# A one-core decoder layer: three query-weight roundings, two inverse roots, the sparse rows and one residual load put at other places in their engines' programs

## The chip, the cores and the metric

The kernel runs on one core of a Trainium2 chip. The metric is the device time of one execution in microseconds (us), the median of several. The core has TensorE (PE in the profile, its weight loads PEld), VectorE (DVE), ScalarE (ACT), GpSimd (POOL) and SyncE (SP), which here only issues DMAs. Each runs its own program in order and waits on semaphores for the others.

## The reference

One layer on 256 tokens of width 2048, float32 throughout. Only the second half matters here:

```python
h = h + concatenate([ret, nsa]) @ w_out[l]
h = h + peer_ffn(rmsnorm(h, norm2_g[l]), peer_wq[l], peer_subkeys[l], peer_u[l], peer_v[l])
return rmsnorm(h, norm_f_g)

def peer_ffn(x, wq, subkeys, u, v):        # x: 256 x 2048
    q = (x @ wq).reshape(n, 8, 2, 128)     # the queries
    s = einsum('nhpd,pkd->nhpk', q, subkeys)
    sv, si = top_k(s, 16)                  # and top 16 of the 16 x 16 sums: 128 experts a token
    hid = gelu(einsum('cd,chkd->chk', x, u[experts]))
    return einsum('chk,chkd->cd', gate * hid, v[experts])
```

u and v hold 16384 rows of 2048 floats each.

## The kernel before

**Weight blocks.** All dense weights arrive as blocks of 1 MB (`raw`, four slots). For an exact product in the fast float format a block is split: ScalarE rounds it into `hi` (`round_static`, `round_lap`; L1072, L1082), VectorE subtracts to get `lo` (`rest_static`, `rest_block`; L1436), and TensorE does three products for each of 16 pieces, 48 matmuls in all (`weights_block`; L585 to L587). `hi` and `lo` have two slots, so the rounding of block m waits until block m - 2 is multiplied (`block_done`). Blocks are numbered through the program: `M_OUT2` (52) begins the second half of the output product, `M_WQ` (60) the 16 blocks of the query weights, `M_PEER` (76) the blocks of u. The text calls the query blocks Q0 to Q15, which are blocks 60 to 75.

**Normalisation.** h is summed up token by token while the output product ends. Its squares are added up and the inverse root is needed in two forms: `rstd`, 128 x 256, made of a TensorE sum over partitions (`spread_sums`, L888, in the middle of Q1), by which VectorE scales each query block's result (`scaled`, L1449) and then h itself (`normalise`, 16 instructions in two groups of 8, L1722); and `rstd_cols`, one column for each half of the tokens, for the 64 sparse tokens. Each takes two activations of ScalarE (`rsqrt`, L1086 and L1088). TensorE may start a query block only when the block two before has been scaled out of its bank (`acc_evacuated`).

**Dense and sparse tokens.** 192 tokens go through all 128 blocks of u and v. For the last 64, GpSimd gathers the chosen rows, and VectorE multiplies them with `xs` (their normalised h) and sums into `acc`; both are filled on partitions 64 to 127 and, from there or by a zero, on 0 to 63. `acc` is set up by a ScalarE copy (L1263) and a VectorE zero (L1731), `xs` by one VectorE instruction (L1733) and a DMA.

**The u blocks of the first half.** 64 blocks of u (`u_block`, L904) are multiplied unsplit. Between blocks 32 and 56 a batch of the gate matrix is built after each (`gate_batch`, L959). After block 60 TensorE opens six banks (L971). ScalarE applies a gelu to each block's result (`hidden_block`, L1273), and after that of block 61 it copies the residual h into the opened banks (L1349, L1351), for which SP has loaded it back from DRAM into `res_back` (L461, L463) where the one-hot tiles of the gate batches stood. Then come 64 blocks of v, split again (`round_split`, L1306; `rest_split`, L1899) and multiplied with the split hidden values `wm` (L1336, L1953, L1954) into all eight banks (`v_block`, L1000 to L1007). The second halves of u and v follow.

**SP's order.** SP asks for the weight blocks in order; the ask for u block r waits until block r - 4 is multiplied. The last lines before the v blocks are:

```python
with sp.Fori(1, HALF // RAW) as lap:
    for s in range(RAW):
        load_after_block(a["u"][RAW * lap + s], RAW * lap + (m_u(0) - RAW + s + 1), s)
sp.wait_ge(gate_rows, BATCHES)
sp.wait_ge(res_stored, 16)
sp.dma_start(res_back[:, 0:1024], res_dram[:, 1024:D]).then_inc(res_loaded, 16)
```

Of the kernel before, what the change touches and what calls it, by code (L numbers as in the profile page):

```python
# [21 lines left out]
ALU = mybir.AluOpType  # L22
ACT = mybir.ActivationFunctionType
AX = mybir.AxisListType

P = 128
T = 256
D = 2048
KT = D // P
# [20 lines left out]
RAW = 4  # L50
# [3 lines left out]
def m_u(half): return M_PEER + 2 * HALF * half  # L54
# [127 lines left out]
def build(nc, a, out):  # L182
    with ExitStack() as ctx:
# [193 lines left out]
        def _(sp):  # L377
# [60 lines left out]
            def load_after_block(src, done, s):  # L438

                sp.wait_ge(block_done, done)  # L440
                sp.dma_start(raw[:, s, :], src).then_inc(raw_loaded[s], 16)
# [6 lines left out]
            for half in range(2):  # L448
                if half:
                    with sp.Fori(0, HALF // RAW) as lap:  # L450
                        for s in range(RAW):
                            load_after_v(a["u"][RAW * lap + (HALF + s)], 2 * RAW * lap + 2 * (HALF - RAW + s + 1), s)
                else:
                    for s in range(RAW):
                        load_after(a["u"][s], M_PEER - RAW + s, s)
                    with sp.Fori(1, HALF // RAW) as lap:
                        for s in range(RAW):
                            load_after_block(a["u"][RAW * lap + s], RAW * lap + (m_u(0) - RAW + s + 1), s)
                    sp.wait_ge(gate_rows, BATCHES)
                    sp.wait_ge(res_stored, 16)  # L460
                    sp.dma_start(res_back[:, 0:1024], res_dram[:, 1024:D]).then_inc(res_loaded, 16)  # L461
                    for x in range(2):
                        sp.dma_start(res_back[TS * x:TS * (x + 1), 1024:3072], res_dram[0:TS, D:2 * D]).then_inc(res_loaded, 16)  # L463

                def load_v(mv, s):
                    if half == 0 and mv < RAW:
                        load_after_block(a["v"][:, mv, :], m_v(0) - RAW + mv + 1, s)
                    else:
                        load_after_v(a["v"][:, mv + HALF * half, :], 2 * (mv + 2 * HALF * half - RAW + 1), s)

                def load_gates(q, g):
                    sp.dma_start(gs[:, g, 0:TD * GROUP_J], gate_dram[q].rearrange("i t j -> i (t j)")).then_inc(gate_loaded[g], 16)

                early = GATED_EARLY // GROUP_J if half == 0 else 0
                first = 0 if half == 0 else HALF // GROUP_J - GATED_EARLY // GROUP_J
                for q in range(early):
                    for r in range(GROUP_J):
                        load_v(GROUP_J * q + r, r % RAW)
                    if q == 1:
                        for s in range(2):  # L480
                            sp.wait_ge(gate_stored[s], 16 * (TD // 32))
                        for g in range(2):
                            load_gates(g, g)
                for q in range(early, HALF // GROUP_J):
                    if half and q == 3:
                        sp.wait_ge(block_done, m_v(1) + 8)
                        sp.dma_start(h_first, res_dram[:, 0:1024]).then_inc(gf_loaded, 16)
                    x = first + q - early
                    if x >= 2:
                        sp.wait_ge(gated, GROUP_J * (x - 1))  # L490
                        load_gates(x, x % 2)
                    for r in range(GROUP_J):
                        load_v(GROUP_J * q + r, r % RAW)
# [17 lines left out]
        def _(pool):  # L511
# [19 lines left out]
            pool.wait_ge(acc_evacuated, M_WQ)  # L531
            pool.dma_start(g2_row[TS:P, :], a["norm2_row"]).then_inc(sparse_loaded, 16)
            pool.dma_start(res_dram, res).then_inc(res_stored, 16)
            pool.wait_ge(xs_ready, 1)
            pool.dma_start(xs[0:TS, :], xs[TS:P, :]).then_inc(sparse_loaded, 16)

            pool.wait_ge(picked_ready, 1)
# [526 lines left out]
        def _(ac):  # L1064
# [9 lines left out]
            def round_static(m):  # L1074
                n = raw_at(m)
                round_block(m, m, n % RAW, n // RAW + 1)
# [7 lines left out]
            def rsqrt(src, dst, width, logged, ready, count, rows=P):  # L1084

                do(dst, src, ACT.Ln, bias=eps[0:rows, :], scale=1.0 / width).then_inc(logged, 1)  # L1086
                ac.wait_ge(logged, count)
                do(dst, dst, ACT.Exp, scale=-0.5).then_inc(ready, 1)  # L1088
# [146 lines left out]
            def square_h(c):  # L1235

                ac.wait_ge(acc_evacuated, M_OUT2 + 2 * c + 2)
                for tt in range(2):
                    at = (2 * c + tt) * 512
                    do(qT[:, at:at + 512], res[:, tt * D + c * 512:tt * D + (c + 1) * 512], ACT.Square,  # L1240
                       accum_out=ss_parts[:, 4 * tt + c:4 * tt + c + 1]).then_inc(sq_ready, 1)
# [13 lines left out]
            for x in range(2):  # L1255
                copy_h(3, x)
                round_h(3, x).then_inc(act_hi_ready, 1)
            square_h(3)
            ac.wait_ge(sq_summed, 2)
            rsqrt(ss_cols, rstd_cols, D, log_ready, rstd_ready, 2)  # L1260
            ac.wait_ge(ss_ready, 2)
            rsqrt(bank[7][:, 0:T], rstd[:, :], D, log_ready, rstd_ready, 3)
            do(acc[TS:P, :], h_sparse, ACT.Copy).then_inc(acc_begun, 1)  # L1263
            for s in range(2, RAW):
                round_static(M_WQ + s)
            with ac.Fori(1, KT // RAW) as lap:
                for s in range(RAW):
                    round_lap(RAW * lap + (M_WQ + s), lap, s, (M_WQ + 8) // RAW + 1)

            def hidden_block(r):  # L1270

# [18 lines left out]
                do(sc[:, 1 - x // 4, 4 * (x % 4):4 * (x % 4) + 4, :].rearrange("p g k -> p (g k)"),  # L1290
                   bank[2 + x % 6][:, :], ACT.Copy).then_inc(q_copied, 1)
            ac.wait_ge(res_stored, 16)
            ac.wait_ge(xs_ready, 1)
            hidden_block(0)

            def round_split(n):
# [134 lines left out]
        def _(dv):  # L1431
# [292 lines left out]
            for s in range(2, RAW):  # L1724
                rest_static(M_WQ + s)
                if s == 2:
                    dv.wait_ge(rstd_ready, 3)
                    scaled(M_WQ, 0, qT[:, 0:T])
                scaled(M_WQ + s - 1, s - 1, qT[:, (s - 1) * T:s * T])
                normalise((0, 8)[s - 2], (8, KT)[s - 2])  # L1730
            vec.memset(acc[0:TS, :], 0.0).then_inc(acc_begun, 1)  # L1731
            dv.wait_ge(sparse_loaded, 16)
            vec.scalar_tensor_tensor(out=xs[TS:P, :], in0=h_sparse, scalar=rstd_cols[TS:P, 1:2], in1=g2_row[TS:P, :],  # L1733
                                     op0=ALU.mult, op1=ALU.mult).then_inc(xs_ready, 1)
            with dv.Fori(1, KT // RAW) as lap:
                for s in range(RAW):
                    rest_block(RAW * lap + (M_WQ + s), s, s)
                    scaled(RAW * lap + (M_WQ + s - 1), s - 1, qT[:, bass.ds(RAW * T * lap + (s - 1) * T, T)])
            scaled(M_PEER - 1, 1, qT[:, (KT - 1) * T:KT * T])

            done = {"route": 0, "items": 0}
# [301 lines left out]
```

## Time and profile before

| | |
|---|---|
| median of 3 runs | 1823.74 us (1823.47 to 1824.27) |
| the profiled execution | 1824.49 us, of which the span of its instructions is 1822.7 us |
| TensorE matmul, weight load | 1787.2 us (98%), 1615.2 us (89%) |
| VectorE, ScalarE, GpSimd | 76%, 42%, 9% of the span |
| mean granted TensorE clock | 0.994 |
| DMA | 531 MB, mean 291 GB/s |

A span is the time from the first to the last instruction. Matmuls overlap: each one's row lasts longer than the distance to the next, so TensorE's rate is read from how many start in a stretch. "Idle before" and the arrow name the instruction or DMA that ended a wait.

### The profile page before, as it was taken

What the parts mean: (1) busy time and instruction counts of PE and PEld (TensorE: products, weight loads), DVE (VectorE), ACT (ScalarE), POOL (GpSimd) and SP (SyncE); (2) the same over time, 40 slices, a digit from 0 to 9 for tenths busy, and PEclk for the clock granted to TensorE, in tenths of its full rate; (3) what the DMA queues carried; (4) which work ended last, traced back from release to release, by engine and by line L of the source; (5) the groups of instructions that cost most, each with busy time, mean ns of one, the idle gap of its engine ahead of it and who ended that gap; (6) DMA issues with size and microseconds to landing.
All of it is one profiled execution on the core that took longest, in us unless ns stands there. A gap on an engine that the chain in (4) does not pass through costs nothing.

```text
span 1822.7 us, 28601 instructions
## 1 busy us (share of the span) xinstructions
PE 1787.2 (98%) x10988; PEld 1615.2 (89%) x10988; DVE 1389.8 (76%) x2156; ACT 770.0 (42%) x1060; POOL 172.2 (9%) x157
## 2 busy tenths in 40 slices
PE   8999999998999999999999999999999999999997
PEld 8999999788899999999977777789999998777775
DVE  6546667565539896887458888989999998998996
ACT  5234445655221101111145555555555555554555
POOL 0000000000000112222210001011111111010110
PEclk9999999999999999999999999999999999999999
DMA  9674443555444898889899999999999999999984
GB/s 350 234 280 160 163 139 116 208 185 201 168 156 167 309 337 317 314 330 341 333 343 368 323 319 329 351 339 368 380 369 376 374 366 346 351 365 361 362 305 151
DMA packets 77136, 531.07 MB, mean 291 GB/s; under 512 B 8796, under 2 KB 9196, under 8 KB 15997
## 3 DMA queue, kind: packets, MB, share of 16 engines
q1 hardware_dynamic: 54080, 377.44, 55.9%
q0 software_dynamic: 22352, 151.59, 22.8%
q8 instruction: 48, 0.79, 0.2%
q10 hardware_dynamic: 620, 0.96, 0.2%
q14 instruction: 36, 0.29, 0.0%
HBM read 512.60 MB, written 15.20 MB: 290 GB/s over the span
## 4 chain that ended last, share of the span: by engine, by line
PE 94%; DVE 2%; DMA 1%; issue 1%; ACT 1%; SPq 0%; ACTq 0%; DVEq 0%
PE bank L904 17%; PE bank L920 11%; PE bank L585 8%; PE bank L586 7%; PE bank L587 7%; PE bank L1001 6%; PE bank L1000 6%; PE bank L1005 6%; PE bank L1006 6%; PE bank L1007 6%; PE bank L921 5%; PE bank L959 2%; DMA raw<-in_v 1%; DVE lo L1436 0%; PE bank L712 0%
## 5 line engine op out<-in xcount | busy, mean ns | idle before, releaser
L1899 DVE TENSOR_TENSOR lo<-raw,hi 128x1024 fp32r<-128x1024 f32 x384 | 463.8, 1222 | 113.4 <-ACT hi L1306 112.9
L1306 ACT ACTIVATE hi<-raw 128x1024 fp32r<-128x1024 f32 x384 | 404.8, 1059 | 325.8 <-PE bank L1007 241.4
L904 PE MATMUL bank<-hT,raw 128*128 128x192 f32 x2048 | 337.5, 326 | 0.0
L904 PEld LDWEIGHTS bank<-hT,raw 128*128 128x128 f32 x2048 | 332.3, 190 | 0.1
L920 PE MATMUL bank<-xr,hi 128*128 128x384 f32 x1024 | 291.3, 359 | 0.0
L1436 DVE TENSOR_TENSOR lo<-raw,hi 128x2048 fp32r<-128x2048 f32 x75 | 171.8, 2291 | 111.2 <-ACT hi L1072 78.9
L921 PE MATMUL bank<-xr,lo 128*128 128x192 f32 x1024 | 256.4, 250 | 0.0
L1000 PE MATMUL bank<-hi,wm 128*128 128x512 f32 x512 | 200.9, 392 | 6.2 <-DVE wm L1954 5.7
L1001 PE MATMUL bank<-lo,wm 128*64 128x512 f32 x512 | 203.6, 398 | 0.0
L1005 PE MATMUL bank<-lo,wm 128*128 128x512 f32 x512 | 201.0, 393 | 0.0
L1006 PE MATMUL bank<-hi,wm 128*128 128x512 f32 x512 | 199.9, 390 | 0.0
L1007 PE MATMUL bank<-hi,wm 128*128 128x512 f32 x512 | 199.9, 390 | 0.0
L585 PE MATMUL bank<-act,hi 128*128 128x256 f32 x672 | 195.4, 291 | 2.1 <-DVE lo L1436 1.9
L921 PEld LDWEIGHTS bank<-xr,lo 128*128 128x128 f32 x1024 | 196.0, 191 | 0.0
L920 PEld LDWEIGHTS bank<-xr,hi 128*128 128x128 f32 x1024 | 192.4, 188 | 0.0
L586 PE MATMUL bank<-act,hi 128*128 128x256 f32 x672 | 191.1, 284 | 0.0
L587 PE MATMUL bank<-act,lo 128*128 128x256 f32 x672 | 191.1, 284 | 0.0
L1771 DVE SCALAR_TENSOR_TENSOR rows_sb<-rows_sb,xs 128x2048 f32<-128x2048 f32 x64 | 146.3, 2286 | 20.0 <-DMA rows_sb<-in_u_rows,pairs 19.8
L1774 DVE SCALAR_TENSOR_TENSOR acc<-rows_sb,wcol,acc 128x2048 f32<-128x2048 f32 x64 | 150.2, 2347 | 9.8 <-DMA rows_sb<-in_v,pairs 9.2
L1273 ACT ACTIVATE arena<-bank 128x192 f32<-128x192 f32 x64 | 21.1, 329 | 285.2 <-PE bank L904 285.2
L585 PEld LDWEIGHTS bank<-act,hi 128*128 128x128 f32 x672 | 129.8, 193 | 6.7 <-issue 6.0
L1000 PEld LDWEIGHTS bank<-hi,wm 128*128 128x128 f32 x512 | 96.7, 189 | 43.8 <-issue 10.0
(296 smaller groups left out, 2629.3 us busy)
## 6 DMA issues: line engine op xcount, KB each, us to landing
raw<-in_u SPq DMA_DIRECT2D x128, 1024.0 KB
raw<-in_v SPq DMA_DIRECT2D x128, 1024.0 KB
raw<-in_w_in SPq DMA_DIRECT2D x44, 1024.0 KB
raw<-in_w_out SPq DMA_DIRECT2D x16, 1024.0 KB
raw<-in_wq SPq DMA_DIRECT2D x16, 1024.0 KB
gate_matrix<-gs POOLq DMA_DIRECT2D x12, 768.0 KB, 12.2
gs<-gate_matrix SPq DMA_DIRECT2D x12, 768.0 KB
raw<-in_cmp_w SPq DMA_DIRECT2D x8, 1024.0 KB
```

The lines of the kernel that those rows point to most:

```text
L585: mm(dst, wh, mh, start=first, stop=False)
L586: mm(dst, wh, ml, start=False, stop=False)
L587: return mm(dst, wl, mh, start=False, stop=last)
L904: last = mm(bank[s % 2][:, 0:TD], raw[:, s, k * P:(k + 1) * P], xn[:, k, 0:TD], start=(k == 0), stop=(k == KT - 1))
L920: mm(acc_bank[:, 0:2 * TD], hi[:, s % 2, w], xr[:, k, :], start=(k == 0), stop=False, skip_group_check=True)
L921: last = mm(acc_bank[:, 0:REST_COLS], lo[:, s % 2, w], xr[:, k, 0:REST_COLS], start=False, stop=(k == KT - 1), skip_group_check=True)
L1000: mm(bank[4 + dc][:, :], packed, vh[:, cols], start=False, stop=False, skip_group_check=True)
L1001: return mm(bank[4 + dc][0:TS, :], packed[:, 0:TS], vl[:, cols], start=False, stop=closing, skip_group_check=True)
L1005: mm(bank[dc][:, :], whole, vl[:, cols], start=opening and dc < 2, stop=False, skip_group_check=True)
L1006: mm(bank[dc][:, :], whole, vh[:, cols], start=False, stop=False, skip_group_check=True)
L1306: do(hi[:, s % 2, cols], raw[:, s, cols], ACT.Copy).then_inc(v_hi_ready, 1)
L1899: vec.tensor_tensor(lo[:, n % 2, cols], raw[:, n % RAW, cols], hi[:, n % 2, cols].bitcast(F32), ALU.subtract).then_inc(v_lo_ready, 1)
```

## The change

ScalarE, between the output product and the query blocks: the rounding of Q2 is put ahead of `rstd`'s root, the rounding of Q3 ahead of `rstd_cols`'s root (which was first), and the copy into `acc` behind all query blocks. VectorE: the zero of `acc` is gone, and `xs` is made in four parts of 512 columns, one behind each of the last four query blocks' roundings and scalings (those four are taken out of the loop). GpSimd writes the zeros. SP asks for the residual after the ask for u block 60 and before those for 61, 62 and 63.

```diff
@@ block.sync
-                    with sp.Fori(1, HALF // RAW) as lap:
+                    with sp.Fori(1, HALF // RAW - 1) as lap:
                         for s in range(RAW):
                             load_after_block(a["u"][RAW * lap + s], RAW * lap + (m_u(0) - RAW + s + 1), s)
+                    load_after_block(a["u"][HALF - RAW], m_u(0) + HALF - 2 * RAW + 1, 0)
                     sp.wait_ge(gate_rows, BATCHES)
                     sp.wait_ge(res_stored, 16)
                     sp.dma_start(res_back[:, 0:1024], res_dram[:, 1024:D]).then_inc(res_loaded, 16)
                     for x in range(2):
                         sp.dma_start(res_back[TS * x:TS * (x + 1), 1024:3072], res_dram[0:TS, D:2 * D]).then_inc(res_loaded, 16)
+                    for s in range(1, RAW):
+                        load_after_block(a["u"][HALF - RAW + s], m_u(0) + HALF - 2 * RAW + s + 1, s)
@@ block.gpsimd
             pool.dma_start(res_dram, res).then_inc(res_stored, 16)
-            pool.wait_ge(xs_ready, 1)
+            nc.gpsimd.memset(acc[0:TS, :], 0.0).then_inc(acc_begun, 1)
+            pool.wait_ge(xs_ready, 4)
             pool.dma_start(xs[0:TS, :], xs[TS:P, :]).then_inc(sparse_loaded, 16)
@@ block.scalar
             square_h(3)
+            round_static(M_WQ + 2)
+            ac.wait_ge(ss_ready, 2)
+            rsqrt(bank[7][:, 0:T], rstd[:, :], D, log_ready, rstd_ready, 2)
+            round_static(M_WQ + 3)
             ac.wait_ge(sq_summed, 2)
-            rsqrt(ss_cols, rstd_cols, D, log_ready, rstd_ready, 2)
-            ac.wait_ge(ss_ready, 2)
-            rsqrt(bank[7][:, 0:T], rstd[:, :], D, log_ready, rstd_ready, 3)
-            do(acc[TS:P, :], h_sparse, ACT.Copy).then_inc(acc_begun, 1)
-            for s in range(2, RAW):
-                round_static(M_WQ + s)
+            rsqrt(ss_cols, rstd_cols, D, log_ready, rstd_ready, 3)
             with ac.Fori(1, KT // RAW) as lap:
                 for s in range(RAW):
                     round_lap(RAW * lap + (M_WQ + s), lap, s, (M_WQ + 8) // RAW + 1)
+            do(acc[TS:P, :], h_sparse, ACT.Copy).then_inc(acc_begun, 1)
@@ block.vector
                 if s == 2:
-                    dv.wait_ge(rstd_ready, 3)
+                    dv.wait_ge(rstd_ready, 2)
                     scaled(M_WQ, 0, qT[:, 0:T])
                 scaled(M_WQ + s - 1, s - 1, qT[:, (s - 1) * T:s * T])
                 normalise((0, 8)[s - 2], (8, KT)[s - 2])
-            vec.memset(acc[0:TS, :], 0.0).then_inc(acc_begun, 1)
-            dv.wait_ge(sparse_loaded, 16)
-            vec.scalar_tensor_tensor(out=xs[TS:P, :], in0=h_sparse, scalar=rstd_cols[TS:P, 1:2], in1=g2_row[TS:P, :],
-                                     op0=ALU.mult, op1=ALU.mult).then_inc(xs_ready, 1)
-            with dv.Fori(1, KT // RAW) as lap:
+            with dv.Fori(1, KT // RAW - 1) as lap:
                 for s in range(RAW):
                     rest_block(RAW * lap + (M_WQ + s), s, s)
                     scaled(RAW * lap + (M_WQ + s - 1), s - 1, qT[:, bass.ds(RAW * T * lap + (s - 1) * T, T)])
+            dv.wait_ge(sparse_loaded, 16)
+            dv.wait_ge(rstd_ready, 3)
+            for s in range(RAW):
+                r = KT - RAW + s
+                rest_block(M_WQ + r, s, s)
+                scaled(M_WQ + r - 1, s - 1, qT[:, (r - 1) * T:r * T])
+                cols = slice(s * 512, (s + 1) * 512)
+                vec.scalar_tensor_tensor(out=xs[TS:P, cols], in0=h_sparse[:, cols], scalar=rstd_cols[TS:P, 1:2], in1=g2_row[TS:P, cols],
+                                         op0=ALU.mult, op1=ALU.mult).then_inc(xs_ready, 1)
```

ScalarE's later wait for `xs_ready` goes from 1 to 4. TensorE's program is the same.

ScalarE, where the output product ends and the query blocks begin, before the change. L1240 squares the last part of h, the pairs L1086 and L1088 are the two roots, L1263 is the copy into `acc`, L1072 the roundings of Q2 and Q3:

```order
L1240 ACTIVATE arena,small<-arena 128x512
L1086 ACTIVATE small<-small 128x2 [waits sq_summed]
L1088 ACTIVATE small<-small 128x2 [waits log_ready]
L1086 ACTIVATE rstd<-bank,small 128x256 [waits ss_ready]
L1088 ACTIVATE rstd<-rstd 128x256 [waits log_ready]
L1263 ACTIVATE acc<-arena 64x2048
L1072 ACTIVATE hi<-raw 128x2048 [waits block_done,raw_loaded2]
L1072 ACTIVATE hi<-raw 128x2048 [waits block_done,raw_loaded3]
```

The same place in the changed kernel, where its lines have other numbers (L1076 rounds, L1090 and L1092 are a root):

```order
L1244 ACTIVATE arena,small<-arena 128x512
L1076 ACTIVATE hi<-raw 128x2048 [waits block_done,raw_loaded2]
L1090 ACTIVATE rstd<-bank,small 128x256 [waits ss_ready]
L1092 ACTIVATE rstd<-rstd 128x256 [waits log_ready]
L1076 ACTIVATE hi<-raw 128x2048 [waits block_done,raw_loaded3]
L1090 ACTIVATE small<-small 128x2 [waits sq_summed]
L1092 ACTIVATE small<-small 128x2 [waits log_ready]
L1269 UNCONDITIONAL_BRANCH
```

Q2's rounding now stands ahead of the wait for `ss_ready`, Q3's between the roots, and no copy follows.

VectorE, from the second group of 8 normalising instructions (L1722) to the first block of the loop (Q4), before:

```order
L1449 TENSOR_TENSOR arena<-bank,rstd 128x256 [waits block_done]
L1722 TENSOR_TENSOR hT<-hT,rstd 128x256 x8
L1731 MEMSET acc 64x2048
L1733 SCALAR_TENSOR_TENSOR xs<-arena,small,g_row 64x2048 [waits sparse_loaded]
L1735 UNCONDITIONAL_BRANCH
L1735 ISA
L1436 TENSOR_TENSOR lo<-raw,hi 128x2048 [waits hi_ready]
```

And changed:

```order
L1453 TENSOR_TENSOR arena<-bank,rstd 128x256 [waits block_done]
L1726 TENSOR_TENSOR hT<-hT,rstd 128x256 x8
L1735 UNCONDITIONAL_BRANCH
L1735 ISA
L1440 TENSOR_TENSOR lo<-raw,hi 128x2048 [waits hi_ready]
```

The zero and the `xs` instruction are gone from between Q3 and Q4; the latter is now four instructions of 64x512 behind Q12 to Q15.

SP, at the end of the first u blocks, before:

```order
L441 DMA raw<-in_u 128x2048
L456 REGISTER_ALU
L456 COMPARE_AND_BRANCH
L461 DMA res_back<-residual 128x1024 [waits res_stored,gate_rows]
L463 DMA res_back<-residual 64x2048 x2
L441 DMA raw<-in_v 128x2048 [waits block_done] x4
```

And changed:

```order
L456 COMPARE_AND_BRANCH
L441 DMA raw<-in_u 128x2048 [waits block_done]
L462 DMA res_back<-residual 128x1024 [waits res_stored,gate_rows]
L464 DMA res_back<-residual 64x2048 x2
L441 DMA raw<-in_u 128x2048 [waits block_done] x3
L441 DMA raw<-in_v 128x2048 [waits block_done] x4
```

The three residual DMAs stand ahead of three asks for u blocks, each of which waits for one more block.

## Rows read from the trace of the kernel before

**Rows 1.** The page, part 4: the chain that ended last, by engine

```profile
PE 94%; DVE 2%; DMA 1%; issue 1%; ACT 1%; SPq 0%; ACTq 0%; DVEq 0%
```

**Rows 2.** TensorE's waits, whole span: us in total, times, longest us

```profile
PE bank L585 <- DVE lo L1436: 6.8, 3, 4.5
PE bank L1000 <- DVE wm L1954: 5.7, 3, 4.5
PE bank L585 <- DVE arena L1449: 4.8, 1, 4.8
```

**Rows 3.** Timeline of TensorE: start us, us, instruction, [idle before]

```profile
448.33 0.55 PE L585 MATMUL bank<-h_parts,hi 128*128 128x256 f32 x1 [4.76 <-DVE arena L1449]
465.90 0.58 PE L585 MATMUL bank<-h_parts,hi 128*128 128x256 f32 x1 [4.47 <-DVE lo L1436]
```

**Rows 4.** Stretches: PE, PEld, DVE, ACT, POOL busy (instructions), clock, DMA, GB/s

```profile
448.40:451.20 2.80, 2.80 (x13) 2.80 (x14) 2.80 (x10) 0.00 (x0) 0.00 (x0) 0.50 0.69 234
466.00:471.80 5.80, 5.80 (x27) 5.80 (x28) 2.19 (x1) 0.00 (x0) 0.00 (x0) 0.50 0.97 345
480.00:528.00 48.00, 48.00 (x402) 48.00 (x401) 22.16 (x17) 16.90 (x9) 0.00 (x0) 1.00 0.54 187
927.40:932.60 5.20, 5.20 (x12) 3.76 (x13) 2.70 (x4) 2.04 (x4) 0.00 (x0) 0.50 1.01 421
1000.00:1030.00 30.00, 30.00 (x133) 23.27 (x132) 23.77 (x35) 15.66 (x21) 1.87 (x2) 1.00 0.91 326
```

**Rows 5.** Timeline of ScalarE around the end of Q1

```profile
440.74 0.47 ACT L1086 ACTIVATE rstd<-bank,small 128x256 f32<-128x256 f32 x1 [3.20 <-PE bank L888]
441.68 1.91 ACT L1263 ACTIVATE acc<-arena 64x2048 f32<-64x2048 f32 x1
443.62 3.71 ACT L1072 ACTIVATE hi<-raw 128x2048 fp32r<-128x2048 f32 x2
```

**Rows 6.** Timeline of VectorE, Q2 to Q4

```profile
445.56 2.29 DVE L1436 TENSOR_TENSOR lo<-raw,hi 128x2048 fp32r<-128x2048 f32 x1 [8.07 <-ACT hi L1072]
...
455.72 0.42 DVE L1449 TENSOR_TENSOR arena<-bank,rstd 128x256 f32<-128x256 f32 x1 [2.32 <-PE bank L587]
456.06 2.77 DVE L1722 TENSOR_TENSOR hT<-hT,rstd 128x256 f32<-128x256 f32 x8
459.18 1.76 DVE L1731 MEMSET acc<- 64x2048 f32 x1 [0.36 <-issue]
460.98 2.35 DVE L1733 SCALAR_TENSOR_TENSOR xs<-arena,small,g_row 64x2048 f32<-64x2048 f32 x1
```

**Rows 7.** Timeline of GpSimd, its last issue before the changed place

```profile
431.85 0.58 POOL L533 DMA_DIRECT2D residual<-arena  x1
```

**Rows 8.** Timeline of TensorE, last u blocks and first v block

```profile
884.88 20.97 PE L904 MATMUL bank<-hT,raw 128*128 128x192 f32 x128
...
927.37 0.77 PE L1000 MATMUL bank<-hi,wm 128*128 128x512 f32 x1 [4.54 <-DVE wm L1954]
```

**Rows 9.** Timeline of ScalarE there

```profile
912.47 0.33 ACT L1273 ACTIVATE arena<-bank 128x192 f32<-128x192 f32 x1 [6.26 <-PE bank L904]
919.51 1.12 ACT L1349 ACTIVATE bank<-res_back 128x512 f32<-128x512 f32 x2 [6.70 <-DMA res_back<-residual]
920.56 2.14 ACT L1351 ACTIVATE bank<-res_back 128x512 f32<-128x512 f32 x4
...
923.23 2.00 ACT L1306 ACTIVATE hi<-raw 128x1024 fp32r<-128x1024 f32 x2 [0.28 <-DMA raw<-in_v]
```

**Rows 10.** SP's issues there

```profile
901.41 0.33 SPq L461 DMA_DIRECT2D res_back<-residual  x1
...
905.88 0.34 SPq L441 DMA_DIRECT2D raw<-in_v  x1
```

**Rows 11.** Two stretches there; columns as in rows 4

```profile
889.00:894.00 5.00, 5.00 (x33) 5.00 (x32) 1.22 (x1) 1.09 (x3) 4.08 (x3) 1.00 0.54 172
901.00:923.00 22.00, 21.84 (x132) 21.28 (x131) 4.69 (x5) 4.12 (x10) 4.91 (x3) 1.00 1.02 390
```

More of the change, by code:

```diff
@@ L1292, in _ @@
             ac.wait_ge(res_stored, 16)
-            ac.wait_ge(xs_ready, 1)
+            ac.wait_ge(xs_ready, 4)
             hidden_block(0)
```

## The prediction

> **What bounds the kernel now.** I read the chain that ended last first: 94% of it is TensorE [rows 1], so only what shortens TensorE's own time or its waits can count. Second, TensorE's waits over the whole span [rows 2]: three kinds, 17.3 us in all, and each kind's longest is nearly all of it: 4.5, 4.5 and 4.8 us. Third, where these three lie [rows 3, 8]: 4.76 us before 448.33 (the start of Q2), 4.47 us before 465.90 (the start of Q4), 4.54 us before 927.37 (the start of the first v block). Sum 13.77 us. Fourth, TensorE's pace behind each [rows 4]. After the first, 13 matmuls start in 2.80 us; after the second, 27 in 5.80; in an undisturbed stretch 402 in 48.00, or 0.119 us each. After the third it is 12 in 5.20 us against 133 in 30.00, or 0.226 each. The granted clock column says why: 0.50 in the three stretches, the lower of the two levels (1.2 against 2.4 GHz), and 1.00 in the others; ahead of each TensorE had stood idle for over 4 us. So every idle stretch has a second price: 2.80 - 13 x 0.119 = 1.25, 5.80 - 27 x 0.119 = 2.59, and 5.20 - 12 x 0.226 = 2.49 us. Sum 6.3 us.
>
> **The start of Q2.** Who is late? VectorE scales Q0 and Q1 out of their banks only behind Q2's `lo` (2.29 us at 445.56), which waits for ScalarE's rounding at 443.62, and that stands behind the root for `rstd` (440.74) and the copy into `acc` (441.68, 1.91 us) [rows 5, 6]. Yet ScalarE sat idle for 3.20 us before 440.74, from 437.54, and Q0, which the rounding waits for, was multiplied by about then: TensorE ended Q1 at 448.33 - 4.76 = 443.57, and a block is 48 x 0.119 = 5.7 us, with four small sums besides. Changed, the rounding (half of 3.71, so 1.9 us) fills that idle time: 437.5 to 439.4. `lo` follows until 441.7, VectorE having been idle since 445.56 - 8.07 = 437.49. `rstd` comes when it did, at 441.68, so Q0 is scaled by 442.2, and TensorE wants to start Q2 at 443.57. The wait of 4.76 us is gone, with its slow stretch.
>
> **The start of Q3 and Q4.** What is late next is VectorE's chain behind each scaling. The rows give it as it was for Q4: scaling from 455.72, eight normalising instructions until 456.06 + 2.77 = 458.83, then a pause of 0.36, the zero (1.76) and `xs` (2.35), and Q4's `lo` after 463.33 [rows 6]. TensorE started 0.28 us after that `lo` ended. Without the zero and `xs` the `lo` goes from 458.83 to 461.12, and TensorE could start at 461.40; it had run out of work at 465.90 - 4.47 = 461.43 [rows 3]. So the second wait closes almost exactly. The same chain now decides Q3 too (ScalarE rounds Q3 from 443.6 to 445.5, VectorE scales, scales Q1 at about 443.8, and 461.12 - 455.72 = 5.4 us on, at 449.2, `lo` is there, just when TensorE is through with Q2). I charge 0.2 us for each of the two. Bounds: nothing, and 0.2 + 0.36 each if the pause before the zero comes with the loop's branch. From Q5 on no normalising is left and VectorE has slack.
>
> **Where the moved work goes.** ScalarE's `rstd_cols` root, two activations on 2 columns, now behind Q3's rounding, is under 1 us before an idle stretch. The copy into `acc` (1.91 us) falls behind Q15's rounding, where ScalarE has nothing to do until TensorE has multiplied Q15 and the first u block. The four parts of `xs` (each about 2.35 / 4 = 0.6 us) follow VectorE's 2.29 + 0.42 in a block of 5.7 us: over 2 us to spare. They cost the path nothing; without that cover 2.4 us. GpSimd now waits for the fourth part before its `xs` DMA, and behind this wait stand the gathers, which need the routing of all 64 tokens, tens of us later. Its zero starts behind the issue at 431.85 [rows 7], with no other work on that engine. No GpSimd arithmetic is in this trace; nearest is VectorE's 1.76 us for the same tile, and I take its effect as zero (see the rivals).
>
> The Trainium skill (SBUF — State Buffer, Who interferes with whom) says that VectorE and GpSimd share a port pair as an exclusive lock: a GpSimd instruction that only writes does not stop a VectorE one with two SBUF inputs, but can hold up `tensor_scalar` in its two-port mode until it is over. No run here shows it. By the first half the sum stands; by the second only the two `tensor_scalar` that prepare the sum for `rstd` could be late, which is the last rival below.
>
> **The first v block.** ScalarE, after the gelu of u block 61 (912.47), waited 6.70 us for the residual, until 919.51, and copied it for 3.2 us, so the gelu of block 62 and the first rounding of v came at 922.6 and 923.23 [rows 9]; from that rounding to TensorE's start it is 927.37 - 923.23 = 4.14 us. TensorE was free at 927.37 - 4.54 = 922.83 [rows 8]. The residual was asked for at 901.41, the first v block at 905.88 and used 17.35 us later [rows 10]. From 901 to 923 the DMA engines are full, at 390 GB/s [rows 11], so these two waited behind other transfers. Changed, SP issues the residual when the last gate batch is done. This is where the run of four u blocks starts, 884.88, each 20.97 / 4 = 5.24 us: at some 885.1, or 16.3 us sooner. Part of its 1.57 MB falls into a stretch where the engines are half idle (889 to 894: 0.54, 172 GB/s).
>
> Is it in time? ScalarE wants it at 912.8; it has 27 us where it took up to 18. Then the copies end at 916.1, block 62's gelu follows its end (922.83 - 5.24 = 917.6) at 917.9, the rounding of v starts at 918.2 and TensorE could start at 922.4, before 922.83, if v has landed by 918.2. Its queue carries u60, residual, u61, u62, u63 and v0, 6.8 MB from 885.1; if gathers and gate stores took half of 390 GB/s all the time it would land at 920; at the full rate it would land some 5 us after its ask, at 911. I take in between, about 915: the gathers do not run all the time. So the third wait of 4.54 us and its slow stretch go. The second v block is then next: its rounding waits for the end of u63 and one gelu, and 3.8 us of splitting stand against 20 x 0.226 = 4.5 us of the first v block; I charge 0.1 us.
>
> **The sum.** 13.77 + 6.33 = 20.1 us off, 0.5 us on. Idle is counted from a matmul's modelled end, about 0.16 us after its successor could have started (0.28 against 0.12), three times, which gives 0.4 back. Net 20.0. The profiled execution took 1824.49 us, 0.75 above the median of the runs, and the waits are the program's, so I take them off the median: 1823.74 - 20.0 = 1803.7 us. TensorE has only 1.2 us of other waits behind 927 [rows 2], so nothing there swallows it.
>
> **Rivals.**
> - The first v block still lands late. For: 17.35 us from ask to use before. Against: the residual no longer stands ahead of it. At the bound of 920 TensorE starts at 924.1, 1.3 us idle, and if the clock falls all the same 2.5 more: 1807.5. Chance 0.13.
> - The chain through Q3 and Q4 is longer than its rows (loop branch, wake-ups), and the clock falls once or twice: some 1 us idle and 2.6 us slow, each: 1807 to 1811. For: the margin is 0.03 us. Against: the 0.36 us ahead of the zero is the only pause inside the chain. Chance 0.10.
> - Given back: the v stage is bound by DMA (share 0.91 from 1000 to 1030 [rows 4]), and starting earlier only waits later: 1823.7. Against: TensorE does not wait there, and a transfer is asked for by blocks done. Chance 0.02.
> - Slower: the zero on GpSimd holds VectorE's preparation of the `rstd` sum. It starts at 432.4; VectorE was done with the preparation at 437.49, TensorE's sum comes at about 440, and `rstd` has 1.5 us more, so it costs nothing up to some 8.6 us and from there us for us. It ends on the slower side only beyond 8.6 + 20, about 29 us, 16 times VectorE's 1.76. At 33 us, say, it would be 1803.7 + 24.4 = 1828.1. Chance 0.02.
>
> A residual queued ahead of u61 could also stall TensorE, but 3.7 MB at half of 390 GB/s is 19 us from 885.1, and u61 is wanted at about 907.
>
> **The numbers.** The forecast holds with 0.73, between 1802 and 1805.5. With the first two rivals the range is 1801.5 to 1811, which leaves out well under 2 in 10. A change of 0.2%, 3.6 us, is what this measurement can tell from none. Faster by more: forecast and first two rivals, 0.96; within: 0.02; slower: 0.02.
>
> **What would show it.** In the changed profile TensorE should have no wait over 1 us between 430 and 930, the granted clock 1.00 in all stretches from there to the end, Q2 start near 443.5, the first u block some 13.6 us sooner than before, ScalarE's copies of the residual start right behind block 61's gelu, and VectorE's `lo` of Q4 directly behind the eight normalising instructions. I am wrong if a wait of some us reappears at Q3, Q4 or the first or second v block, or if a low clock shows without a wait before it.

## The result and the profile after

The changed kernel takes 1803.72 us (median of 4 runs, 1802.99 to 1805.51) against 1824.01 us (4 runs, 1823.47 to 1824.36) on the same chip: ratio 0.989, interval 0.9873 to 0.9908, 20.3 us less. The profiled execution took 1804.10 us, its span is 1802.3 us, its mean granted clock 0.998.

TensorE's waits over the whole span, as in [rows 2] (us in total, times, longest):

```profile
PE bank L675 <- DMA arena<-in_window_tables: 7.1, 1, 7.1
PE bank L589 <- DVE arena L1453: 2.0, 1, 2.0
PE bank L1004 <- DVE wm L1963: 1.2, 2, 0.6
...
PE bank L589 <- DVE lo L1440: 0.4, 1, 0.4
```

The three waits of 4.5 to 4.8 us are gone. The first line is a wait at the start, which stood at 6.7 before; the second is one of 1.9 to 2.0 us at 66 us, which was among the 6.8 of [rows 2] and was left alone.

ScalarE at the end of Q1, as in [rows 5] (start, duration, instruction, idle before):

```profile
437.64 1.92 ACT L1076 ACTIVATE hi<-raw 128x2048 fp32r<-128x2048 f32 x1 [0.69 <-PE bank L591]
440.90 0.47 ACT L1090 ACTIVATE rstd<-bank,small 128x256 f32<-128x256 f32 x1 [1.35 <-PE bank L892]
441.41 0.42 ACT L1092 ACTIVATE rstd<-rstd 128x256 f32<-128x256 f32 x1
443.83 1.92 ACT L1076 ACTIVATE hi<-raw 128x2048 fp32r<-128x2048 f32 x1 [2.01 <-PE bank L591]
```

Q2's rounding fills the idle time ahead of the root. The root starts at 440.90 where it was 440.74, but so does all around it in this execution (VectorE's row at 430.36 now stands at 430.52), so the root is not held up. VectorE there, as in [rows 6]:

```profile
439.58 2.29 DVE L1440 TENSOR_TENSOR lo<-raw,hi 128x2048 fp32r<-128x2048 f32 x1 [1.92 <-ACT hi L1076]
441.86 0.42 DVE L1453 TENSOR_TENSOR arena<-bank,rstd 128x256 f32<-128x256 f32 x1
443.77 0.42 DVE L1453 TENSOR_TENSOR arena<-bank,rstd 128x256 f32<-128x256 f32 x1 [1.49 <-PE bank L591]
444.11 2.77 DVE L1726 TENSOR_TENSOR hT<-hT,rstd 128x256 f32<-128x256 f32 x8
446.79 2.29 DVE L1440 TENSOR_TENSOR lo<-raw,hi 128x2048 fp32r<-128x2048 f32 x1
449.53 0.42 DVE L1453 TENSOR_TENSOR arena<-bank,rstd 128x256 f32<-128x256 f32 x1 [0.45 <-PE bank L591]
449.87 2.77 DVE L1726 TENSOR_TENSOR hT<-hT,rstd 128x256 f32<-128x256 f32 x8
452.55 2.29 DVE L1440 TENSOR_TENSOR lo<-raw,hi 128x2048 fp32r<-128x2048 f32 x1
```

`lo` follows the eight normalising instructions at once. From scaling to the end of `lo` the chain is 449.08 - 443.77 = 5.31 us, against the predicted 5.4; the 0.36 us pause ahead of the zero did not come with the loop's branch.

The second place: SP's issues, as in [rows 10], then ScalarE, as in [rows 9], and TensorE, as in [rows 8]:

```profile
869.80 0.34 SPq L441 DMA_DIRECT2D raw<-in_u  x1
871.58 0.33 SPq L462 DMA_DIRECT2D res_back<-residual  x1
...
876.78 10.73 SPq L441 DMA_DIRECT2D raw<-in_u  x3
892.38 17.30 SPq L441 DMA_DIRECT2D raw<-in_v  x4
```

```profile
898.96 0.33 ACT L1277 ACTIVATE arena<-bank 128x192 f32<-128x192 f32 x1 [6.24 <-PE bank L908]
899.19 1.11 ACT L1353 ACTIVATE bank<-res_back 128x512 f32<-128x512 f32 x2
900.23 2.15 ACT L1355 ACTIVATE bank<-res_back 128x512 f32<-128x512 f32 x4
904.16 0.33 ACT L1277 ACTIVATE arena<-bank 128x192 f32<-128x192 f32 x1 [1.79 <-PE bank L908]
904.39 1.99 ACT L1310 ACTIVATE hi<-raw 128x1024 fp32r<-128x1024 f32 x2
```

```profile
893.73 15.60 PE L908 MATMUL bank<-hT,raw 128*128 128x192 f32 x95
909.47 0.47 PE L1004 MATMUL bank<-hi,wm 128*128 128x512 f32 x1
```

The residual copies stand right behind block 61's gelu, and the first v matmul has no listed wait. But VectorE is not as it was; the rows that its items of the sparse tokens wait for come later:

```profile
889.23 2.35 DVE L1783 SCALAR_TENSOR_TENSOR acc<-rows_sb,wcol,acc 128x2048 f32<-128x2048 f32 x1 [12.50 <-DMA rows_sb<-in_v,pairs]
899.94 2.29 DVE L1780 SCALAR_TENSOR_TENSOR rows_sb<-rows_sb,xs 128x2048 f32<-128x2048 f32 x1 [8.36 <-DMA rows_sb<-in_u_rows,pairs]
...
904.19 2.29 DVE L1780 SCALAR_TENSOR_TENSOR rows_sb<-rows_sb,xs 128x2048 f32<-128x2048 f32 x1 [1.95 <-DMA rows_sb<-in_u_rows,pairs]
...
906.41 2.36 DVE L1908 TENSOR_TENSOR lo<-raw,hi 128x1024 fp32r<-128x1024 f32 x2
...
908.89 0.22 DVE L1963 TENSOR_TENSOR wm<-arena,wm 128x64 fp32r<-128x64 f32 x1
```

Before, the same three items began at 898.74, 907.98 and 912.48, the last of them with block 61's gelu (912.47 in [rows 9]); now the last begins 5.2 us behind that gelu (898.96), and the first `lo` of v waits for VectorE itself. `wm` ends at 909.11, and the first v matmul starts 0.36 us behind it. That is the distance in the runs in which TensorE waits for it (927.01 to 927.37 before), so there is no slack left here, though no wait is listed: waits are counted from modelled ends, and the last u matmul's is 909.33. Where `wm` is ready sooner (the changed kernel measured again, below), the first v matmul starts 0.29 us ahead of that end and not 0.14 us behind it. By this comparison, an estimate, some 0.4 us are lost here.

### The profile page after: what moved, and what is told of

Same layout as the page of the kernel before. It is cut to its first block, busy times and chain, and to the rows that moved or that the text cites. A ratio compares the mean times of both kernels' runs of the same rounds, so it can differ in the third digit from the quotient of the medians.

```text
span 1802.3 us, 28580 instructions
## 1 busy us (share of the span) xinstructions
PE 1780.0 (99%) x10988; PEld 1608.9 (89%) x10988; DVE 1389.0 (77%) x2158; ACT 770.1 (43%) x1060; POOL 174.1 (10%) x158
## 4 chain that ended last, share of the span: by engine, by line
PE 96%; DVE 2%; issue 1%; ACT 1%; DMA 0%; SPq 0%; ACTq 0%; DVEq 0%
PE bank L908 18%; PE bank L924 11%; PE bank L589 8%; PE bank L590 7%; PE bank L591 7%; PE bank L1005 6%; PE bank L1004 6%; PE bank L1009 6%; PE bank L1010 6%; PE bank L1011 6%; PE bank L925 5%; PE bank L963 2%; PE bank L716 0%; PE bank L942 0%; PE bank L769 0%
## 5 line engine op out<-in xcount | busy, mean ns | idle before, releaser
L1076 ACT ACTIVATE hi<-raw 128x2048 fp32r<-128x2048 f32 x55 | 105.0, 1909 | 66.7 <-PE bank L591 57.5
```

## The experiments

The kernel before took 1824.5 us (9 runs) on the chip of the first four, 1825.74 (9) on that of the next four, and 1823.97 (7) on that of the last three.

**The query part alone.** The changed kernel with SP's order as before:

```diff
-                    with sp.Fori(1, HALF // RAW - 1) as lap:
+                    with sp.Fori(1, HALF // RAW) as lap:
...
-                    for s in range(1, RAW):
-                        load_after_block(a["u"][HALF - RAW + s], ...)
```

> The changed kernel with the residual asked for as before, behind the last u block; only ScalarE's, VectorE's and GpSimd's edits stand. My theory (three independent waits, two of them at the start of Q2 and Q4): both query waits and their slow-clock stretches are gone, 4.76 + 4.47 + 1.25 + 2.59 + 0.3 less 0.4, so 13.0 us under before, 1811.0 us; the wait of 4.5 us before the first v block and its slow stretch stay. Rival (given back: work saved early is lost again at the crowded DMA queue before the v stage): less than 10 us, with a v wait grown beyond 5 us. Second rival (the gathers, not the residual, hold the first v block up): same time as my theory, but VectorE's last gathered item before the v blocks comes where it did relative to the u blocks.

1809.5 us (5 runs, 1809.11 to 1811.51), ratio 0.9921 (0.9908 to 0.9935): 15.0 us less. TensorE's waits behind `wm`:

```profile
PE bank L1001 <- DVE wm L1960: 5.7, 3, 4.6
```

The query waits are gone and that of the first v block stands. It came out 1.5 us faster than expected. Around the wait, in the profiled execution (1809.36 us), the low clock shows in 913.9 to 917.3, 3.4 us, all of it with TensorE at work. In the kernel before it lasted 6.8 us (925.9 to 932.7), but TensorE started only at 927.37, so 5.3 us of it counted. Stretches, columns as in [rows 4]:

```profile
913.50:917.50 4.00, 4.00 (x12) 2.96 (x11) 2.70 (x4) 1.44 (x4) 0.00 (x0) 0.57 1.00 418
917.50:921.00 3.50, 3.50 (x17) 2.70 (x16) 1.48 (x2) 2.15 (x3) 0.00 (x0) 1.00 1.04 433
```

Half of 5.3 less 3.4 us is an estimated 0.9 us of the gap. Another 0.4 us are the query terms of 1.25 and 2.59, which were too small (see the slow stretches below). The five times fall into 1809.1 to 1809.5 and 1811.3 to 1811.5. Whether the length of the low clock makes these two groups is not shown: only one of the five was profiled.

**The residual part alone.** The kernel before with the new order of SP's issues and nothing else.

> The kernel before with only the residual's ask moved ahead of u blocks 61 to 63. My theory: the v wait of 4.54 us and the slow stretch of 2.49 go, 0.1 comes, so 6.9 us under before, 1817.0 us; both query waits stay, with the clock at 0.50 behind each. Rival (the two parts help each other): the sum of this run's and the query part's gain is off the 20.3 us of both by over 1.5 us. In the profile I look for the gathers: with the residual in the queue earlier, VectorE's last two gathered items should come about 5 us later against the u blocks than before, as in the changed kernel, and the first v block's lo behind them within 0.3 us of TensorE's need.

1817.89 us (5 runs, 1817.05 to 1818.07), 0.9962 (0.9948 to 0.9976): 6.6 us less. With the 15.0 above that is 21.6; the whole change gave 20.3 and, measured again, 21.35. The parts add up as far as these runs can tell: each interval above is some 5 us wide. Both query waits stand in its profile, 4.5 and 4.8 us at the longest. VectorE ahead of the first v block:

```profile
902.55 2.35 DVE L1777 SCALAR_TENSOR_TENSOR acc<-rows_sb,wcol,acc 128x2048 f32<-128x2048 f32 x1 [12.66 <-DMA rows_sb<-in_v,pairs]
913.31 2.29 DVE L1774 SCALAR_TENSOR_TENSOR rows_sb<-rows_sb,xs 128x2048 f32<-128x2048 f32 x1 [8.41 <-DMA rows_sb<-in_u_rows,pairs]
...
917.32 2.29 DVE L1774 SCALAR_TENSOR_TENSOR rows_sb<-rows_sb,xs 128x2048 f32<-128x2048 f32 x1 [1.71 <-DMA rows_sb<-in_u_rows,pairs]
```

Block 61's gelu is at 912.13 here, so the last item begins 5.2 us behind it, as in the changed kernel; with the query part alone it began 0.1 us behind (898.36 against 898.25). The earlier residual is what makes the gathered rows late.

**ScalarE's order alone.** The kernel before with the new order of roundings and roots; the zero and `xs` stay on VectorE between Q3 and Q4.

```diff
+            round_static(M_WQ + 2)
             ac.wait_ge(ss_ready, 2)
-            for s in range(2, RAW):
-                round_static(M_WQ + s)
+            rsqrt(bank[7][:, 0:T], rstd[:, :], D, log_ready, rstd_ready, 2)
+            round_static(M_WQ + 3)
```

> The kernel before with only ScalarE's order changed (roundings of Q2 and Q3 first, copy into acc last); VectorE still zeroes acc and makes xs in one piece between Q3 and Q4. My theory: the wait before Q2 (4.9 with the modelled end) and its slow stretch (1.25) go; the one before Q4 stays at 4.5 to 4.7 us, since 0.36 + 1.76 + 2.35 = 4.47 us of VectorE work stand before Q4's lo, with 2.6 us of slow clock: 6.2 us under before, 1817.6 us. Rival (the two query waits are one lateness handed on, so that curing the first cures part of the second): 9 to 13 us under before.

1817.0 us (4 runs, 1816.51 to 1818.55), 0.9961 (0.9945 to 0.9976). Q2's wait alone is gone; that of the first v block is 3.9 us here instead of 4.5. Q4's stays, and VectorE shows what holds it:

```profile
452.44 1.76 DVE L1731 MEMSET acc<- 64x2048 f32 x1 [0.37 <-issue]
454.24 2.35 DVE L1734 SCALAR_TENSOR_TENSOR xs<-arena,small,g_row 64x2048 f32<-64x2048 f32 x1
456.62 2.29 DVE L1436 TENSOR_TENSOR lo<-raw,hi 128x2048 fp32r<-128x2048 f32 x1
```

**The zero back on VectorE.** The changed kernel with the zero where it stood.

```diff
-            nc.gpsimd.memset(acc[0:TS, :], 0.0).then_inc(acc_begun, 1)
...
+            vec.memset(acc[0:TS, :], 0.0).then_inc(acc_begun, 1)
             with dv.Fori(1, KT // RAW - 1) as lap:
```

> The changed kernel with the zero of acc back on VectorE between Q3 and Q4 instead of on GpSimd. My theory of the margin (Q4's lo has under 0.3 us to spare): TensorE waits 1.76 + 0.36 = 2.1 us more before Q4. If the clock stays at its upper level through a wait of 2.1 us the time is 1803.7 + 2.1 = 1805.8 us; if it falls as it did behind the waits of over 4 us, 2.6 more: 1808.4 us. Rival (VectorE has slack there): 1803.7 us, no wait.

1807.34 us (4 runs, 1806.75 to 1808.18), 0.9906 (0.9891 to 0.9922), so 3.6 us over the changed kernel (3.1 if each is taken against the kernel before on its own chip). Of that 1.9 us is the wait it brings back ahead of Q4 (TensorE's timeline), behind which the clock stayed high (second stretch). The rest need not be the zero's: the profiled execution, the fastest of the four, had its low clock at 67.3 to 70.7 (first stretch), behind the old wait at 66 us, where neither the kernel before nor the changed one showed any.

```profile
458.19 0.38 PE L588 MATMUL bank<-h_parts,hi 128*128 128x256 f32 x1 [1.91 <-DVE lo L1439]
```

```profile
67.40:70.60 3.20, 3.20 (x17) 3.20 (x17) 0.80 (x1) 0.00 (x0) 0.00 (x0) 0.50 1.02 383
458.40:461.40 3.00, 3.00 (x26) 3.00 (x26) 2.15 (x1) 0.00 (x0) 0.00 (x0) 1.00 0.78 227
```

**The changed kernel again.**

> The changed kernel itself once more, beside the variants of this call and to see how its own runs scatter (1802.99 to 1805.51 us so far). If the scatter is the clock's (a low stretch that follows a wait of 2 us near 66 us in some executions and not in others), single runs lie at about 1803.5 or 1.5 to 2 us above, and the profile shows a stretch at 0.50 only where the run is above. If it is the first v block's, which had 0.2 us to spare, slower runs have a wait there.

1804.39 us (4 runs, 1803.49 to 1804.98), 0.9885 (0.987 to 0.99). The profiled execution (1804.38 us) shows neither cause named above: the clock is 1.00 behind the wait at 66 us, and the first v matmul (909.72) is 0.56 us behind `wm`, so not held by it. What spreads the runs over 1.5 us stays open.

```profile
908.94 0.22 DVE L1963 TENSOR_TENSOR wm<-arena,wm 128x64 fp32r<-128x64 f32 x1
909.72 0.53 PE L1004 MATMUL bank<-hi,wm 128*128 128x512 f32 x1
```

**The zero eight times.** GpSimd writes the zeros eight times, each after the last.

```diff
+            for x in range(7):
+                nc.gpsimd.memset(acc[0:TS, :], 0.0).then_inc(osq_ready, 1)
+                pool.wait_ge(osq_ready, x + 2)
             nc.gpsimd.memset(acc[0:TS, :], 0.0).then_inc(acc_begun, 1)
```

> The changed kernel with GpSimd writing the zeros eight times over, one after the other (8 x 1.83 us, from 432.6 to about 447.5), so that they lie beside VectorE's two small instructions on one SBUF input (437.2), the scaling and the normalising. My theory: VectorE's instructions keep their lengths and the time is 1803.7 us. Rival (the shared port pair as an exclusive lock, as in the Trainium skill's page SBUF — State Buffer, Who interferes with whom): the two tensor_scalar each wait for up to one zero, 1.8 us, the sum for rstd comes up to 2.4 us later than at 440.9, and TensorE waits up to 1 us before Q2: 1804 to 1806 us.

1803.38 us (4 runs, 1803.02 to 1804.34), 0.9881 (0.9865 to 0.9896): no cost. Its GpSimd, and VectorE in 432 to 446 by groups (line, operation, count, busy us, mean ns, idle before):

```profile
432.49 13.04 POOL L538 MEMSET acc<- 64x2048 f32 x7
445.58 1.80 POOL L540 MEMSET acc<- 64x2048 f32 x1
```

```profile
L1443 DVE TENSOR_TENSOR lo<-raw,hi 128x2048 fp32r<-128x2048 f32 x2 | 4.6, 2293 | 1.5 <-ACT hi L1079 1.5
L1729 DVE TENSOR_TENSOR hT<-hT,rstd 128x256 f32<-128x256 f32 x6 | 2.1, 418 | 0.0
L1724 DVE TENSOR_SCALAR wmt<-base,small 128x128 f32<-128x128 f32 x2 | 1.1, 994 | 0.0
```

The instructions with two inputs in SBUF take what they took alone (2293 and 418 ns; 2293 and 420 in the changed kernel). The two `tensor_scalar` that prepare the `rstd` sum take 994 ns on average against 285 and end at 438.2 us, just when the third of the eight zeros, begun at 436.24, is over. This is what the Trainium skill (SBUF — State Buffer, Who interferes with whom) says of both kinds; the trace agrees. In the changed kernel the one zero ran from 432.60 to 434.43 and these two started at 437.18, so there they did not meet. The hold costs nothing: VectorE then waits for ScalarE until 439.47 in any case, and the root for `rstd` starts at 440.79, no later than without the seven extra zeros (440.90).

**The residual one block later.** Asked for behind the ask for u block 61 in place of 60.

```diff
-                    load_after_block(a["u"][HALF - RAW], ...)
+                    for s in range(2):
+                        load_after_block(a["u"][HALF - RAW + s], ...)
```

> The changed kernel with the residual asked for one weight block later (behind the ask for u block 61, so two blocks sooner than before instead of three). My theory: it is wanted behind block 61's gelu, some 22 us after this ask, and takes 10 to 17: no new wait, 1803.7 us; the gathered rows that come in while it is loaded move too, so VectorE's last two items before the v blocks shift by up to 5 us against those of the changed kernel. Rival (each block counts: the queue is full, and the first v block lands later by what the residual is later): TensorE waits 1 to 3 us before the first v block, 1805 to 1808 us.

1809.58 us (5 runs, 1805.95 to 1809.91), 0.991 (0.9896 to 0.9923). The expectation was wrong; the rival named in it (each block counts) fits the profiled execution and its wait of 1.2 us. In that execution (1805.95 us) the residual is in time, but the v block that is queued behind it is not:

```profile
907.31 2.00 ACT L1311 ACTIVATE hi<-raw 128x1024 fp32r<-128x1024 f32 x2 [1.89 <-DMA raw<-in_v]
```

```profile
911.46 0.46 PE L1005 MATMUL bank<-hi,wm 128*128 128x512 f32 x1 [1.21 <-DVE wm L1964]
```

It is rounded 7.4 us behind block 61's gelu (899.89), against 5.4 in the changed kernel. VectorE's last item still begins 4.6 us behind that gelu (904.49). Three runs took a further 3.7 us; none of them was profiled, so why stays open.

**The row items one block later.** The 24 items of this stage are spread over one more weight block (`HALF - 3` for `HALF - 4`, line 88).

> The changed kernel with the pace of the gathers in u blocks 32 to 60 stretched by one block, so that the last gathered item before the v blocks is asked for one block (5.2 us) later. In the changed kernel's profile VectorE did that item until 906.5 us and the first v block's lo behind it until 908.8, with TensorE's need at 909.3. My theory: this item, and no longer the residual or the first v block's landing, is what comes last there, so TensorE now waits 3 to 6 us before the first v block, with a low clock behind it of 1.5 to 2.6 us: 1808 to 1812 us. Rival (there is slack; VectorE's wait for the item is filled otherwise): 1803.7 us.

1808.98 us (4 runs, 1807.7 to 1810.29), 0.9913 (0.9898 to 0.9928). The size is as expected, the mechanism is not: TensorE waits 0.9 us for the first v block and 2.8 us for a weight block of u, and the clock stays at 1.00 behind both. Its waits, then the place:

```profile
PE bank L908 <- DMA raw<-in_u: 2.8, 1, 2.8
```

```profile
896.33 8.88 PE L908 MATMUL bank<-hT,raw 128*128 128x192 f32 x53 [2.77 <-DMA raw<-in_u]
```

VectorE's last item begins at 905.40, only 1.2 us later than in the changed kernel, and the first `lo` of v waits for ScalarE's rounding, which waits for the landing. So here the weight loads come last, not the item. The mean share of the DMA engines does not foretell it: in 865 to 875 it is 0.98 where the changed kernel has 0.73, but it is 0.98 in the next experiment too, which has no wait for a u block.

**The row items two blocks sooner.** `HALF - 6`.

> The changed kernel, with the 24 row items of its second stage spread over weight blocks that end two blocks sooner, so that VectorE's last items before the first v block fall sooner. If VectorE's last item is what now comes last ahead of the first v block (it ended at 906.41 us, and TensorE could first go on at 909.3 us), then this has no wait to take away but gives the place slack: 1803.5 us, scatter no larger than in the changed kernel, the item ends by about 901 us, and the first v block starts at block 61's end. If it is the transfers as a whole that are just in time there (the 16 DMA engines read 1.00 to 1.02 from 875 us on), asking for rows sooner pushes back the u blocks instead: a wait for a u weight block appears, 1 to 3 us, and the time is 1805 to 1808 us.

1803.91 us (4 runs, 1803.24 to 1805.77), 0.9889 (0.9873 to 0.9906): no change. VectorE's last item is done at 893.74, and then it idles until v has been rounded, which now waits for the landing:

```profile
907.19 2.00 ACT L1310 ACTIVATE hi<-raw 128x1024 fp32r<-128x1024 f32 x2 [1.66 <-DMA raw<-in_v]
```

TensorE waits 1.0 us. Of the first theory the item and the time came true, but not the start without a wait; the wait for a u block of the second did not come. With the items out of the way the landing of v ends last. It comes at 907.2, where in the changed kernel v was there by 904.4 (0.8 us of the difference stand ahead of the last u blocks already). So rows asked for sooner seem to push back a load, as the second theory has it, but v's and not one of u. The profiled execution, the slowest of the four, again had a low clock at 67.1 to 70.5.

**Four additions moved to GpSimd.** The changed kernel with half of the eight additions that VectorE makes at 59.77 us given to GpSimd, which is idle before and makes them as soon as their inputs are there, at 41.79 us.

```diff
-                    for kind in range(2):
+                    for kind in range(1):
...
+            for g in range(GROUPS):
+                pool.wait_ge(acc_evacuated, VC + g + 1)
+                for lh in range(2):
+                    nc.gpsimd.tensor_tensor(blk[:, 1, ...], rows_of[...], pe_cols[...], ALU.add)
```

> The changed kernel, with four of the eight additions that VectorE makes at 59.77 us (3.95 us for the eight) made by GpSimd. In every profile so far TensorE waits 1.9 us at about 66 us for the low part of the weight block that VectorE makes behind them. If these additions are the cause, half of them gone brings that low part 1.97 us sooner and the wait goes: 1801.8 us (1801.2 to 1802.5). If the weight block is held by something else (ScalarE's high part at 64.33 us, or the transfer), the time stays at 1803.7 us and the wait is there with another releaser. If GpSimd slows VectorE, which works beside it there, the low parts between 60 and 70 us read longer than 2.29 us each and less is gained.

1801.9 us (4 runs, 1801.38 to 1802.4), 0.9878 (0.9862 to 0.9895): 22.1 us faster than the kernel before and, against the 1803.4 to 1804.4 of the changed kernel and its equals, about 2 us faster. The intervals of the ratios overlap; what bears the 2 us out is that all four runs are shorter than any of the changed kernel's, and that a wait of this length is gone.

VectorE there, and TensorE's waits:

```profile
60.13 2.03 DVE L1541 TENSOR_TENSOR arena<-arena,wmt 128x240 f32<-128x240 f32 x4
62.08 2.29 DVE L1449 TENSOR_TENSOR lo<-raw,hi 128x2048 fp32r<-128x2048 f32 x1
```

```profile
PE bank L598 <- DVE lo L1449: 0.4, 1, 0.4
```

Of the waits for `lo` only one of 0.4 us is left, which was there before; the one at 66 us is gone. GpSimd's four took 4.37 us and were done by 46.2 us, so whether GpSimd slows VectorE at 60 us was not tried.

**Both.**

> The two edits before this one together. They touch places 800 us apart and share no engine's queue in between, so the gains should add: 1801.6 us if the row items cost nothing sooner, or 2 us under what the kernel with sooner items alone gives.

1803.55 us (4 runs, 1802.49 to 1804.82), 0.9889 (0.9873 to 0.9906). They do not add: the time is 0.4 us under that of the sooner items alone, where 2 us were expected. A new wait stands ahead of 697.21 us, in a gate batch, behind VectorE:

```profile
PE bank L961 <- DVE arena L1870: 1.6, 1, 1.6
```

VectorE made what TensorE needs there behind an item whose rows landed at 694.09. With the sooner items alone that item begins at 690.59 and there is no such wait, so items closer together do not explain it by themselves. TensorE also comes to this place sooner: it could have gone on at 695.58, and in the changed kernel it came at 697.85. Why the rows landed when they did was not tried.

## Why the prediction was right

The time, the way and the three waits came out as forecast; two steps held less well than the time does.

- **Q2.** Right in each time: rounding from 437.64 (437.5 predicted), Q0 scaled by 442.3, no wait. The kernel with ScalarE's order alone shows this wait goes by that order and no other part.
- **Q3 and Q4.** Right: the chain behind a scaling is 5.31 us, and no wait is listed. That the two closed almost exactly is borne out by the zero back on VectorE, which brings back 1.91 us of wait for 1.76 us of work and its pause. The 0.2 us charged twice did not show.
- **Moved work.** Free. The four parts of `xs` and the copy into `acc` left no wait; no run put them alone on the path.
- **GpSimd's zero.** Free: it is over (434.43) before VectorE's preparation starts (437.18). The rival needs one zero of over 8.6 us; it took 1.83. Eight in a row, 14.8 us in all, cost nothing either, though two VectorE instructions were held for the rest of one zero (1.1 us in place of 0.5). One zero as long as the rival's was not run.
- **The first v block.** The two links that the step looked at held: it was rounded at 904.39, which is 917.9 less the 13.5 us that all stands earlier, beside the predicted 918.2. But TensorE started it at 909.47, or 923.0 on the same scale, where 922.4 was predicted. The step did not ask what the residual's 1.57 MB displaces: the gathered rows came some 5 us later, VectorE's last item held back `lo`, and the predicted 0.4 us of slack became a loss of about 0.4 us. That the rows were not later still is luck, as the prediction had not looked at them.
- **The slow stretches.** Right in kind, a little small in size. The stretches of [rows 4] all end inside the low clock. From TensorE's restart to the first matmul that begins at the old pace it is 14 starts in 3.12 us (448.33 to 451.45), 28 in 6.09 (465.90 to 471.99) and 13 in 5.53 (927.37 to 932.90). By the prediction's own paces that makes 1.45, 2.76 and 2.59 us, 6.8 in place of 6.33. The sum would then be 20.5: 13.77 + 6.8 + 0.4, less the 0.1 charged and the 0.4 lost at v. The measured 20.3 us, 21.35 when the changed kernel was run again, and the 21.6 of the two parts cannot tell 20 from 21: the interval of the ratio reaches from 16.8 to 23.2 us.
- **The signs.** From 430 to 930 us no wait over 1 us is listed. The first u block is 13.4 us sooner (536.65 for 550.08). The clock is 1.00 until TensorE's last matmul; it falls to 0.50 only in the last 6 us, where TensorE has nothing to do, as in the kernel before.

## What to carry to other kernels

Here, removing an idle stretch of TensorE of over 4 us was worth half as much again, since the granted clock fell around each. When a transfer is asked for sooner into engines that are nearly full, look for the transfers of other queues that it moves back, and who waits for those. A row without a listed wait is not yet a row with slack: compare its distance to what released it with a row that did wait. When several chains end within 1 us of each other, what ends last changes with every edit: giving one of them slack gained nothing here (1803.91 us), while taking some away cost 5.2 and 4.6 us (the residual and the row items one block later, against the changed kernel on the same chip).

## What was not expected of the hardware

- The low clock that goes with a wait of 3.9 to 4.8 us lasted 3.4 us in three cases and 6.8 us in five (the profiled executions of the kernel before and of the first three experiments), and both lengths occur at the same place of nearly the same program: 3.4 us at Q2 in the kernel before, 6.8 us with the residual part alone. It also began anywhere from 1.7 us before TensorE went on (457.5 for 459.19, at Q4 with ScalarE's order alone) to 0.6 us after (467.4 for 466.78, at Q4 with the residual part alone), and what falls into the wait costs nothing.
- Behind the wait of 1.9 to 2.0 us at 66 us it showed in two of the profiled executions (67.3 to 70.7 and 67.1 to 70.5 us) and not in nine others with the same instructions and the same wait there. What this costs was not settled: the one was the slowest of its kernel's runs (1805.77 against 1803.24 to 1804.41), the other the fastest of its (1806.75 against up to 1808.18).
- A GpSimd zero of 64 x 2048 floats took 1.80 to 1.83 us, as VectorE's (1.76). While one ran, a VectorE `tensor_scalar` was held (994 for 285 ns) and a `tensor_tensor` was not.
